# The last two expert units' rows stay on chip, and their tokens' output rows are stored over finished tiles

## What is computed

```python
    for gi in range(N_EXPERT_GROUPS):
        sl = slice(gi * EXPERTS_PER_GROUP, (gi + 1) * EXPERTS_PER_GROUP)
        gu = jnp.einsum('td,edf->tef', ht, w_gu[sl])
        g_act, up = jnp.split(gu, 2, axis=-1)
        act = jax.nn.silu(g_act) * up * combine[:, sl, None]
        out = out + jnp.einsum('tef,efd->td', act, w_dn[sl])
...
        x = x + hier_moe(h, w_rg[l], b_rg[l], w_re[l], b_re[l], w_e_gu[l], w_e_dn[l])
    return _rmsnorm(x, norm_final)
```

## Time and profile before

| | |
|---|---|
| median of 3 runs | 1193.43 us (1193.3 to 1196.03) |
| profiled execution | 1192.7 us, its span 1190.9 us |
| TensorE busy | 1116.9 us, 94% of the span |
| VectorE, ScalarE, GpSimd busy | 537.8, 351.6, 131.5 us |
| moved by DMA | 196.35 MB, 165 GB/s on the mean |
| chain that ended last | TensorE 75%, VectorE 11%, issue 4%, ScalarE 3% |

### The profile page before, as it was taken

One profiled execution on the slowest core, in us unless ns is written; L12 is line 12 of the kernel. 1 busy time (PEld: TensorE's weight loads), 2 busy tenths in 40 slices (PEclk: granted clock), 3 DMA queues, 4 the chain that ended last, 5 costly groups with the idle time before them and its releaser, 6 DMA issues.

```text
span 1190.9 us, 16483 instructions
## 1 busy us (share of the span) xinstructions
PE 1116.9 (94%) x6487; PEld 615.0 (52%) x6487; DVE 537.8 (45%) x1196; ACT 351.6 (30%) x676; POOL 131.5 (11%) x154
## 2 busy tenths in 40 slices
PE   6999999999999899897799999999999999997886
PEld 6545744444844689775474444456643333332232
DVE  6876233334399544796572222335532121211116
ACT  4114631111676332204664100265301111100004
POOL 2000012220000000001100000132011111111004
PEclk9999999999999999999899999999999999999998
DMA  8111022131112452420114000462349999999958
GB/s 284 36 58 53 22 74 78 55 98 48 34 59 110 191 146 68 171 101 1 73 70 177 0 1 1 147 255 99 131 170 347 410 397 426 420 423 425 407 195 335
DMA packets 65973, 196.35 MB, mean 165 GB/s; under 512 B 24444, under 2 KB 41056, under 8 KB 55392
## 3 DMA queue, kind: packets, MB, share of 16 engines
q1 hardware_dynamic: 59184, 178.25, 39.4%
q0 software_dynamic: 6656, 16.95, 3.8%
q10 hardware_dynamic: 48, 0.01, 0.0%
HBM read 167.38 MB, written 33.05 MB: 168 GB/s over the span
## 4 chain that ended last, share of the span: by engine, by line
PE 75%; DVE 11%; issue 4%; ACT 3%; DMA 1%; POOL 0%; DVEq 0%; SPq 0%; POOLq 0%; ACTq 0%
PE bank L2643 20%; PE bank L1554 13%; PE bank L1610 8%; PE bank L1577 6%; PE bank L1672 2%; PE bank L1625 2%; PE bank L2770 2%; PE bank L1540 1%; PE bank L805 1%; PE bank L916 1%; PE bank L866 1%; PE bank L1692 1%; PE bank L853 1%; PE bank L884 1%; DVE arena L756 1%
## 5 line engine op out<-in xcount | busy, mean ns | idle before, releaser
L2643 PE MATMUL bank<-arena 128*128 128x512 f32 (+3 forms) x1032 | 357.4, 506 | 6.6 <-ACT arena L2147 5.4
L2643 PEld LDWEIGHTS bank<-arena 128*128 128x128 f32 x1032 | 196.4, 192 | 161.6 <-issue 140.7
L1554 PE MATMUL bank<-arena 128*32 128x512 f32 x1344 | 152.4, 606 | 14.6 <-issue 13.7
L1554 PEld LDWEIGHTS bank<-arena 128*32 128x32 f32 x1344 | 46.4, 112 | 116.7 <-issue 116.7
L1610 PE MATMUL bank<-arena 128*128 128x512 f32 x220 | 95.6, 592 | 0.0
L1327 DVE TENSOR_TENSOR arena<-arena,bank 128x256 f32<-128x256 f32 x21 | 8.9, 422 | 158.3 <-ACT arena L1213 122.6
L1577 PE MATMUL bank<-arena 128*32 128x512 f32 x672 | 76.5, 595 | 2.4 <-ACT arena L1217 1.4
L2147 ACT ACTIVATE arena<-bank 128x512 f32<-128x512 f32 (+1 forms) x57 | 28.5, 505 | 164.4 <-PE bank L2643 163.9
L1370 DVE TENSOR_TENSOR arena<-arena,bank 128x512 f32<-128x512 f32 x32 | 22.0, 689 | 100.1 <-PE bank L1610 79.5
L1610 PEld LDWEIGHTS bank<-arena 128*128 128x128 f32 x220 | 41.3, 190 | 49.7 <-issue 49.7
L1213 ACT ACTIVATE arena<-bank 128x256 f32<-128x256 f32 x21 | 8.1, 384 | 165.7 <-PE bank L1554 165.7
(11 more groups left out here) (411 smaller groups left out, 1585.8 us busy)
## 6 DMA issues: line engine op xcount, KB each, us to landing
arena<-in_w_e_gu SPq DMA_DIRECT2D x26, 2048.0 KB, 14.3
arena<-in_w_e_dn SPq DMA_DIRECT2D x32, 1024.0 KB, 15.0
arena<-in_w_in SPq DMA_DIRECT2D x11, 1024.0 KB, 5.2
arena<-y_d SPq DMA_DIRECT2D x8, 1024.0 KB, 11.1
arena<-hz_d SPq DMA_DIRECT2D x4, 1792.0 KB, 8.9
arena<-in_w_e_gu SPq DMA_DIRECT2D x6, 1024.0 KB, 13.1
arena<-in_w_e_gu SPq DMA_DIRECT2D x12, 512.0 KB, 14.3
pk_d<-arena SPq DMA_DIRECT2D x8, 640.0 KB, 2.9
```

The costliest lines, as they stand in the source:

```text
L1554: ins = mm(bank[part, :], hgT[:, k, part], w_gu(es[i] % NB, k), start=(k == 0), stop=(k == KT - 1))
L2643: ins = mm(psum[PROJ_BANKS[u % 3]][0:rows, 0:n], lhs(k), rhs(k), start=(k == 0), stop=(k == kt - 1))
```

## The change

The last two units (19 and 20) no longer scatter their rows; these stay in `ysb`. The rest of the tail starts before they are done:

- y_d is cleared in the first 160 us (`clear_rows`), since the slots of late rows are not written. x2 is also stored to DRAM (x2_d), and so are the weights (w_d).
- Behind the scatter of unit 18, SP reads the tiles of y_d back (`sp_rows`), which now holds zeros for the late rows, to other buffers.
- For each row tile ScalarE scales the first expert's rows by their weight ("first"), GpSimd adds x2, VectorE adds the second expert's rows ("sum"). ScalarE squares and roots, VectorE scales ("scale"), and SP stores the tile. Some of these steps stand between the steps of units 19 and 20.
- The late rows' tokens are made apart, as two more row tiles NT and NT + 1: GpSimd gathers their rows of x2 and of their other expert; TensorE adds the late rows by a product with a 0/weight matrix, which also adds two late rows of one token (`pe_late`); VectorE adds these up ("other", "sum") and scales. When all 8 tiles are stored, GpSimd stores these rows over them, by index (L2091).
- The indices, the matrix and its weights are worked out by small operations in units 3 to 9 (`late_indices`, `late_equal`, `late_sums`, `late_tokens`, `late_counts`, `late_weights`).
- The overflow branch now stands behind the tail.

```diff
+        LATE = 2
+        late_u = [UN - LATE + i for i in range(LATE)]
...
-        yg = [view(i * TK * D, TK, D) for i in range(6)] + [view(o_g2 + i * TK * D, TK, D) for i in range(2)]
-        y_out = [view(o_g1 + i * D, D) for i in range(NT)]
+        yg = [view(o, TK, D) for o in (EW, EW + TK * D, EW + 2 * TK * D, o_g1, o_g1 + TK * D, o_g3,
+                                       o_g1 + 2 * TK * D, o_g1 + 3 * TK * D)]
+        assert all(e % NB in (0, 1, 3, 4) for u in late_u for e, _i in BLOCKS[4 * u:4 * u + 4])
+        xr = [view(o, D) for o in (o_tmp + 6 * D, o_cx)]
+        yo = hg
+        row_sq = view(o_tmp + 2 * D, D)
...
+                sp.wait_ge(s["t_m_e"], 2 * (m + 1))
+                sp.dma_start(x2_d[m * P:(m + 1) * P, :], x2[:, m]).then_inc(s["t_x2"], 16)
                 sp.wait_ge(s["t_xn"], 16 * (m + 1))
...
-            sp.wait_ge(s["t_r_dve"], 4)
+            sp.wait_ge(s["t_r_dve"], 6)
+            sp.dma_start(w_d.rearrange("(m p k) o -> p m (k o)", p=P, k=TK), w_mk).then_inc(s["t_xn"], 16)
+            sp.wait_ge(s["t_x2"], X2_STORED)
+            sp.dma_start(fin_g, a["norm_final"].unsqueeze(0).to_broadcast([P, D])).then_inc(s["t_x2"], 16)
             sp_experts(sp, moe, 0)
+            sp_rows(sp, 0)
...
+                    if isinstance(p, int):
+                        for step in ACT_BESIDE.get(u, ()):
+                            act_rows(act, 0, *step)
                     act.wait_ge(q["dn"], UN * p + u)
...
+                    if u == 3:
+                        late_indices(dve, v, link)
+                    if u == 6:
+                        late_equal(dve, v, link)
+                    if u == 9:
+                        late_sums(dve, v, link)
+                    for step in DVE_BESIDE.get(u, ()):
+                        dve_rows(dve, v, link, 0, *step)
...
+                if u == 4 and isinstance(p, int):
+                    late_tokens(pe, mm)
+                if u == 7 and isinstance(p, int):
+                    late_counts(pe, mm)
...
+                if u == 3 and isinstance(p, int):
+                    late_weights(pool, last_y)
+                if u >= 1 and not (isinstance(p, int) and u - 1 in late_u):
                     wait(q["y"], 2 * UN * p + 2 * u)
-                    pool.indirect_dma_start(y_d, bass.IndirectOffsetOnAxis(ap=ix_sc[:, u - 1:u], axis=0),
-                                            ysb[(u - 1) % 2], None, bounds_check=last_y, oob_is_err=False
-                                            ).then_inc((q["st0"], q["st1"])[(u - 1) % 2], 16)
+                    scatter(pool, q, u - 1, last_y)
...
+            pool_late(pool, moe, last_row, last_y)
+            for step in POOL_STEPS[0]:
+                pool_rows(pool, 0, last_row, *step)
             with overflow(pool):
+                pool.wait_ge(s["l_w"], L_OUT + 16 * (LATE + len(BY_POOL)))
+                for u in late_u:
+                    scatter(pool, moe, u, last_y)
...
+        ORDER = ((0, 1, 2, 3, NT, 4, NT + 1, 5, 6, 7), tuple(range(NT)))
+        L_W = 16 * 4 * CT
+        L_OUT = L_W + 64 * LATE
+        ACT_BESIDE = {UN - 1: [("first", 0)], UN: [("first", 1), ("square", 0), ("first", 2)]}
+        ACT_AFTER = ([("first", 3), ("square", 1), ("first", 4), ("square", 2), ("first", 5), ("square", 3),
+                      ("square", NT), ("first", 6), ("square", 4), ("square", NT + 1), ("first", 7),
+                      ("square", 5), ("square", 6), ("square", 7)],
+                     [st for i in range(NT) for st in (("first", i), ("square", i))])
...
+        POOL_STEPS = ([("first", i) for i in range(NT)] + [("store", i) for i in LATE_ROWS], [("first", i) for i in range(NT)])
+        DVE_BESIDE = {UN - 1: [("sum", 0), ("sum", 1)]}
+        DVE_AFTER = ([("scale", 0), ("sum", 2), ("other", NT), ("other", NT + 1), ("scale", 1), ("sum", 3),
+                      ("scale", 2), ("sum", NT), ("scale", 3), ("sum", 4), ("scale", NT), ("sum", NT + 1),
+                      ("scale", 4), ("sum", 5), ("scale", NT + 1), ("sum", 6), ("scale", 5), ("sum", 7),
+                      ("scale", 6), ("scale", 7)],
...
+        def pool_late(pool, q, last_row, last_y):
+            pool.wait_ge(s["l_w"], L_W + 32 * LATE)
+            pool.wait_ge(s["t_x2"], X2_STORED)
+            pool.wait_ge(q["gu"], UN - 1)
+            for l in range(LATE):
+                at = slice(late_u[l], late_u[l] + 1)
+                pool.indirect_dma_start(xr[l], None, x2_d, bass.IndirectOffsetOnAxis(ap=ix_ga[:, at], axis=0),
+                                        bounds_check=last_row, oob_is_err=False).then_inc(s["l_w"], 16)
+            pool.wait_ge(s["l_w"], L_W + 48 * LATE)
+            pool.wait_ge(q["tr"], 2 * UN)
+            for i in range(2):
+                pool.wait_ge((q["st0"], q["st1"])[(UN - LATE - 1 - i) % 2], rows_of(UN - LATE - 1 - i))
+            for l in range(LATE):
+                pool.indirect_dma_start(yo[l], None, y_d, bass.IndirectOffsetOnAxis(ap=ix_ot[:, l:l + 1], axis=0),
+                                        bounds_check=last_y, oob_is_err=False).then_inc(s["l_w"], 16)
+
+        def pe_late(pe, mm):
+            pe.wait_ge(moe["y"], 2 * UN)
+            pe.wait_ge(s["t_m_rc"], NT + 1)
+            for l in range(LATE):
+                for hf in range(2):
+                    for of in range(LATE):
+                        ins = mm(psum[6 * l + hf][:, :], lt_S[:, of, l], ysb[late_u[of] % 2][:, hf * HALF:(hf + 1) * HALF],
+                                 start=(of == 0), stop=(of == LATE - 1))
+                ins.then_inc(s["f_p"], 1)
...
+        def act_rows(act, r, what, i):
+            if what == "first":
+                y_wait(act, i, r)
+                nc.scalar.activation(yg[i][:, 0], yg[i][:, 0], ACT.Copy,
+                                     scale=wts[:, 0, i:i + 1]).then_inc(s["t_m_pt"], 1)
+                return
+            j = place_of(r, i)
+            c = slice((G4 + j) % 4, (G4 + j) % 4 + 1)
+            act.wait_ge(s["f_c"], j + 1)
+            act.wait_ge(s["xs_r"], G4 + j - 3)
+            nc.scalar.activation(row_sq, sum_of(i), ACT.Square, accum_out=ss[:, c]).then_inc(s["t_q_e"], 1)
+            act.wait_ge(s["t_q_e"], CT * NHALF + j + 1)
+            nc.scalar.activation(rms[:, c], ss[:, c], ACT.Sqrt, bias=epsc[:, 0:1],
+                                 scale=1.0 / D).then_inc(s["rms_r"], 1)
...
+        def pool_rows(pool, r, last_row, what, i):
+            if what == "first":
+                pool.wait_ge(s["t_m_pt"], 2 * NT + NT * r + i + 1)
+                nc.gpsimd.tensor_tensor(yg[i][:, 0], yg[i][:, 0], x2[:, i], ALU.add).then_inc(s["t_m_dg"], 1)
+                return
+            pool.wait_ge(s["xs_r"], G4 + place_of(r, i) + 1)
+            if i in LATE_ROWS:
+                l = LATE_ROWS.index(i)
+                if l == 0:
+                    pool.wait_ge(s["l_w"], L_OUT)
+                    pool.wait_ge(s["f_ot"], 16 * (3 + len(BY_SP)))
+                index = ix_st[:, l:l + 1]
...
+            pool.indirect_dma_start(out, bass.IndirectOffsetOnAxis(ap=index, axis=0), row_out(i), None,
+                                    bounds_check=last_row, oob_is_err=False).then_inc(s["l_w"], 16)
...
+        def dve_rows(dve, v, link, r, what, i):
+            if what == "sum" and i in LATE_ROWS:
+                l = LATE_ROWS.index(i)
+                dve.wait_ge(s["f_p"], l + 1)
+                for hf in range(2):
+                    cols = slice(hf * HALF, (hf + 1) * HALF)
+                    ins = v.tensor_tensor(xr[l][:, cols], xr[l][:, cols], psum[6 * l + hf][:, :], ALU.add)
+                    ins.then_inc(s["f_c"], 1) if hf == 1 else link(ins)
+            elif what == "sum":
+                dve.wait_ge(s["t_m_dg"], NT + NT * r + i + 1)
+                v.scalar_tensor_tensor(yg[i][:, 0], yg[i][:, 1], wts[:, 1, i:i + 1], yg[i][:, 0], ALU.mult,
+                                       ALU.add).then_inc(s["f_c"], 1)
+            elif what == "other":
+                l = LATE_ROWS.index(i)
+                dve.wait_ge(s["l_w"], L_W + 64 * LATE)
+                link(v.scalar_tensor_tensor(xr[l], yo[l], w_ot[:, l:l + 1], xr[l], ALU.mult, ALU.add))
+            else:
+                j = place_of(r, i)
+                c = slice((G4 + j) % 4, (G4 + j) % 4 + 1)
+                if j == 0:
+                    dve.wait_ge(s["t_x2"], X2_STORED + 16)
+                dve.wait_ge(s["rms_r"], G4 + j + 1)
+                link(v.reciprocal(rms[:, c], rms[:, c]))
+                v.scalar_tensor_tensor(row_out(i), sum_of(i), rms[:, c], fin_g, ALU.mult,
...
+                if r == 0 and m == 0:
+                    sp.wait_ge(moe["dn"], UN - LATE)
+                    for i in range(2):
+                        sp.wait_ge((moe["st0"], moe["st1"])[(UN - LATE - 1 - i) % 2], rows_of(UN - LATE - 1 - i))
...
+            for m in BY_SP if r == 0 else range(NT):
+                sp.wait_ge(s["xs_r"], G4 + place_of(r, m) + 1)
```

(14 more changed lines are left out.)

201 lines of the change are left out of this document (111 added, 90 removed).

## The result

The changed kernel takes 1212.96 us (median of 4 runs) where the kernel before takes 1193.37 beside it: 1.0151 times as long (95% interval 1.0122 to 1.018). So it is slower by 15 to 20 us; the forecast was 13.7 us and the range ended at 1214. The profiled execution has a span of 1212.2 us for 1190.9, and the forecast span was 1204.6.

What follows compares the result with a forecast made beforehand. DMA read-back bounds the old tail; in the new one VectorE's list and turns end at 1193.9; plus 2.9, 5.1, 2.0 and 0.7 gives span 1204.6, +13.7 over 1190.9, so 1207 us; range 1191 to 1214.

Steps and rivals of the forecast that it cites:

- VectorE's run: Tail, behind VectorE's last copy: its list of sums, scalings and reciprocals takes 28.4 us if nothing stops it, ending at 1182.4.
- the turns: Tail: VectorE's two-operand operations and GpSimd's x2 additions exclude each other, adding 11.5 us (bounds 0 and 14.1).
- the port costs nothing: Rival, tail: GpSimd's additions run beside VectorE, giving 1195.5 us, within 0.3% of before; chance 0.15.
- The tail follows the reads: Rival, tail: y_d reads bind before and after, so the tail moves 14 us with them, giving 1186.5 us; chance 0.12.
- Tile 0 late: Rival, start of tail: gathers share DMA with the first reads, ScalarE holds unit 20 up to 4 us longer: 1211; chance 0.1.
- Here ScalarE's order decides: Start of tail: scaling of tile 0 delays unit 19's copy, unit 20's product ends at 1150.8, VectorE's last copy at 1154.0.
- the branch's 2.0 us: End of program: the overflow branch, now behind SP's last wait, costs 2.0 us (bounds 0.5 and 3.24).
- the forecast's own signs of being wrong: Long VectorE operations missing, VectorE ending before 1182, or TensorE's last gate/up product moved by over 2 us.
- All of it I cost at nothing: Before the tail: clears, x2_d and weight stores, norm_final load, small operations, products and gathers are covered, costing nothing.
- The weight store, the norm_final load and SP's later wait stand before SP's next expert load at 887.76: Start of expert stage: these are covered, as that load waits for the first gate/up product; cost nothing.
- The end: Behind VectorE's end: last tile landing 2.9 us, two indirect stores 5.1, branch 2.0, close 0.7; 10.7 us in all.
- The clears: First 160 us: 8 MB of y_d clears behind chunk loads 4 to 7 cost nothing; bound 0 to 2 us.

Runs made afterwards that it cites:

- no_adds: Changed kernel without GpSimd's eight additions of x2, VectorE's sum waiting for ScalarE's scaling directly (output lacks x2): 1199.23 us, 1.0036 of the kernel before.
- experiments 1 and 2: Changed kernel with GpSimd's x2 additions left out (1199.23 us), or replaced by copies of x2's tile onto itself (1202.01 us) or by memsets (1199.66 us).
- copies_first: Changed kernel with ScalarE's and VectorE's copies of the last two units ahead of all row steps of the tail: 1215.76 us, 1.0179 of the kernel before.
- after_again: The changed kernel itself, unedited, run once more on another occasion: 1210.39 us, 1.0125 of the kernel before.
- start_late: Changed kernel with the w_d store and norm_final load moved behind SP's expert loads of units 0 and 1: 1208.52 us, 1.0113 of the kernel before.
- no_branch: Changed kernel without the branch on the overflow flag and the overflow passes: 1208.34 us, 1.0114 of the kernel before.
- small_late: Changed kernel with the index and mask steps, TensorE's eight small products and the weight gathers moved to units 15 to 18: 1209.27 us, 1.0113 of before.
- rebuilt: Changed kernel with TensorE sums for tiles 2 to 7, indexed stores for tiles 5 to 7, start_late's and small_late's moves: 1197.25 us, 1.0023 of before.
- gather_stores: Changed kernel with tiles 5 to 7 stored by GpSimd with an index that skips the late rows: 1207.51 us, 1.01 of the kernel before.
- rebuilt_2: rebuilt with tile 4's products earlier, sum 1 behind VectorE's last copy, and tile 4 also stored by index: 1195.7 us, 1.0013 of the kernel before.

## Why the prediction came out

The sum forecast a span of 1204.6 and the trace has 1212.2. Of the 7.6 us that were missing 6.6 lie ahead of the scatter of unit 18 (2.7 ahead of the last xn_d store, 2.8 in A, 1.1 in C), which the forecast left where it was, and 1.5 at the end; D was 0.5 shorter than forecast. The direction and the mechanism were right. That the time fell inside the range, 1 us from its upper end, is in part luck: that end had been set for a late tile 0 and for VectorE's bounds, and not for what filled it.

**What was right.** The step that decided it, VectorE's run, held: 28.4 us without stops (27.5 measured in no_adds) and 11.5 for the turns (11.1 measured as the difference of the two runs). From the scatter of unit 18 to VectorE's end the forecast had 63.6 us, the trace has 63.1. The long operations beside a lone addition end 1.07 to 1.08 us after it, as read off. The rival "the port costs nothing" is refuted by experiments 1 and 2. "The tail follows the reads" asked for VectorE done by 1180.2, 49.9 us behind the scatter of unit 18, and with the additions that took 63.1. Without them it takes 49.8 (no_adds), right at the mark where the forecast saw neither gain nor loss, and the loss of 0.4% that stays there stands in A and E. "Tile 0 late" came true in part: the first tile was ready at 1152.2, 7.0 us after its issue and not 5.7, and ScalarE's copy of unit 20 was held 4.1 us; copies_first shows that doing without such holds, by that order, gains nothing.

**Terms that were right for another reason.** I took an addition at 2.35 us, from a multiplication in the earlier trace rows, and six turns with it. An addition takes 2.00 alone, and five operations were lengthened, four by 1.7 us and one by 2.0; waits for additions, which the sum had not, made up the rest. And "Here ScalarE's order decides" does not fit the start of the tail: its scaling of tile 0 was to hold the copy of unit 19, 2.6 us in all. It did not, because that unit's product ended only at 1154.3, 17.4 us after the scatter of unit 18 for 13.1 before; unit 20's gate/up product had come late and run slowly ahead of it. (In after_again, where that product took 8.77, the scaling cost 0.4 at most: unit 20's down product ended at 21.5 there and at 21.0 in copies_first.) In the sum the two errors nearly cancel: VectorE's last copy was to end 23.7 us after that scatter and ended 24.5 after it, of which copies_first, without any row step ahead, still has 21.8. This part of the agreement in D is luck. So is some of the end: the branch's 2.0 us, which are not there, stood in for a landing priced about 2 us too low.

**What was wrong.** One of the forecast's own signs of being wrong came true: TensorE's last gate/up product moved by 8.0 us (1131.56 to 1139.58), where 2 were allowed. 2.7 of them lie ahead of the last xn_d store, 2.8 in A, 1.1 in C (0.4 in after_again) and 1.4 between the scatter of unit 18 and the product. "All of it I cost at nothing" failed for one item, and with the end this left the sum 1 to 6 us short of the 15 to 20 measured. "The weight store, the norm_final load and SP's later wait stand before SP's next expert load at 887.76" is true of SP's queue, but the first gathers of tokens go through the same DMA engines at that time, on GpSimd's queue: 2.8 us in A, and gone when the two DMAs are moved (start_late). The end was short by 1.5: from VectorE's end to the first late store it was 3.9 for 2.9, and from there to the end of the span 8.3 for 7.8 (5.1, 2.0 and 0.7). In that second part the branch, taken at 2.0, costs nothing (no_branch), and the stores themselves took 2.5 us more than the 5.8 they were given with the close. Of the other items two held. The clears cost 0.0: from the first chunk load to the first pk_d store it is 139.67 us (25.92 to 165.59) and was 139.66. The small products take 2.9 us and not 1, but the waits do give them back (small_late). What the x2_d stores cost between 825 and 860 us can't be told from the spread of that stage, and no run left them out. Why TensorE's unit 20 comes 1.4 us later behind the scatter in most of the changed kernels was not tried either.

## What to carry to other kernels

When reads are moved ahead of a stage's end, the tail is as long as its busiest engine's list; price that list first, with every operation that runs beside another engine's. An addition put on GpSimd to relieve VectorE may relieve nothing while VectorE's own operations have two SBUF operands: here the additions cost VectorE's run 11.1 us, where six operations more of its own would be 7.7 by an estimate from their 1.28 us (no run did that). Look for long and short lengths of one instruction, and for ends that follow the other engine's by a fixed time. And "before the next load of this queue" is no cover for a DMA when another queue's gather is due on the same DMA engines.

## What the runs showed of the hardware that I had not expected

An indirect DMA's instruction on GpSimd is held by VectorE as well. In rebuilt, beside a scaling from 1178.34 to 1179.62:

```profile
1178.34 1.28 DVE L2148 SCALAR_TENSOR_TENSOR arena<-arena,rms,levT 128x1024 f32<-128x1024 f32 x1
1178.70 1.81 POOL L2114 DMA_INDIRECT out<-arena  x1 [26.80 <-DMA out<-arena]
...
1180.82 0.97 POOL L2114 DMA_INDIRECT out<-arena  x1 [0.31 <-issue]
```

It took 1.81 us for 0.97 and ended 0.89 us after VectorE's; in the same profile two more took 1.20 and 1.32 us, and in gather_stores two took 1.65 and 1.75, and all ended 0.83 to 0.89 us after VectorE's. One that began 0.1 us ahead of VectorE's scaling in gather_stores was not held (0.97), nor was one in rebuilt_2 that began 0.05 us behind it (0.98). VectorE's own length did not change in rebuilt. Here it cost 0.8 us on GpSimd's queue.

A second thing: the last indirect store takes 6.9 us from its start to the end of the span in the changed kernel and 7.5 in rebuilt (1185.23 to 1192.7), where the last direct store had 5.3 from VectorE's end in before. The last scatter of before had landed in 4.1 us, which was the price I had used; why a store at the very end takes longer was not tried.
